# RWKV-7 scan with the tokens of two products stacked on 128 rows, the backward direction's stack in reverse order

## What is computed

```
def _wkv7_step(S, inp):
    r_t, w_t, k_t, v_t, aa_t, bb_t = inp
    sa = jnp.einsum('zbhij,zbhj->zbhi', S, aa_t)
    S = S * w_t[..., None, :] + sa[..., :, None] * bb_t[..., None, :] + v_t[..., :, None] * k_t[..., None, :]
    y = jnp.einsum('zbhij,zbhj->zbhi', S, r_t)
    return S, y
```

## Time and profile before

| | |
|---|---|
| median of 3 runs | 4864.06 us (4861.78 to 4869.06) |
| the profiled execution | 4869.98 us, its span 4867.9 us |
| busy shares over the span | PE 89%, PEld 74%, DVE 40%, ACT 27%, POOL 26% |
| matmul records in all | 50312 |
| the scan | first `lora` at 2491.8 us, last `y_products` at 3607.7 us |
| mean granted PE clock | 0.954 of 2.4 GHz |

### The profile page before, as it was taken

The page is one execution under the profiler, slowest core; times in us unless marked ns, Lnnn a source line. Parts: engine busy times, 40 slices in busy tenths (PEclk is TensorE's granted clock), DMA queues, the critical chain, the costliest instruction groups (busy, mean ns, idle before and its releaser), DMA issues. The chain is left out here.

```text
span 4867.9 us, 112762 instructions
## 1 busy us (share of the span) xinstructions
PE 4311.4 (89%) x50312; PEld 3614.9 (74%) x50312; DVE 1928.2 (40%) x3380; ACT 1292.7 (27%) x2542; POOL 1279.7 (26%) x794
## 2 busy tenths in 40 slices
PE   3899898999999996996958888888878999999997
PEld 2688856888888885885847777777755888888886
DVE  3011054154252443226146666666633244242441
ACT  1111065211011112236124444444422211011110
POOL 2111032311111115111125454555512311111110
PEclk8899999999999997998979999999989999999998
DMA  3211242311313112121232222221222311313214
GB/s 130 65 59 55 69 134 73 119 39 53 107 40 105 56 58 80 69 78 43 85 89 67 67 68 72 63 74 56 63 100 87 126 35 50 111 40 100 65 50 161
DMA packets 402639, 372.41 MB, mean 77 GB/s; under 512 B 63057, under 2 KB 370513, under 8 KB 399985
## 3 DMA queue, kind: packets, MB, share of 16 engines
q1 hardware_dynamic: 390320, 354.75, 23.6%
q10 hardware_dynamic: 11840, 10.49, 0.6%
HBM read 257.68 MB, written 107.48 MB: 75 GB/s over the span
## 5 line engine op out<-in xcount | busy, mean ns | idle before, releaser
L422 POOL TENSOR_TENSOR f_wlow<-f_raw,f_whigh 128x1024 fp32r<-128x1024 f32 (+1 forms) x152 | 360.1, 2369 | 1671.2 <-ACT f_whigh L493 1671.2
L478 PE MATMUL f_ps<-fx_hh,f_whigh 128*128 128x512 f32 (+1 forms) x2112 | 529.6, 359 | 0.0
L478 PE MATMUL f_ps<-fx_hl,f_whigh 128*128 128x512 f32 (+1 forms) x2112 | 528.5, 358 | 0.0
L478 PE MATMUL f_ps<-fx_hh,f_wlow 128*128 128x512 f32 (+1 forms) x2112 | 528.2, 358 | 0.0
L493 ACT ACTIVATE f_whigh<-f_raw 128x1024 fp32r<-128x1024 f32 (+1 forms) x152 | 156.6, 1030 | 922.7 <-PE f_ps L478 895.0
L478 PEld LDWEIGHTS f_ps<-fx_hl,f_whigh 128*128 128x128 f32 x2112 | 348.7, 189 | 65.8
L478 PEld LDWEIGHTS f_ps<-fx_hh,f_whigh 128*128 128x128 f32 x2112 | 348.5, 189 | 65.6
L478 PEld LDWEIGHTS f_ps<-fx_hh,f_wlow 128*128 128x128 f32 x2112 | 348.2, 188 | 65.7
L478 PE MATMUL f_ps<-mo_oh,f_whigh 128*128 128x512 f32 (+1 forms) x1440 | 360.8, 359 | 26.2 <-POOL f_wlow L422 26.2
L1605 PE MATMUL sc_inv_ps<-sc_tf,sc_bl 64*64 64x64 f32 x6400 | 283.0, 223 | 105.3 <-DVE sc_tf L1956 59.8
L478 PE MATMUL f_ps<-mo_ol,f_whigh 128*128 128x512 f32 (+1 forms) x1440 | 360.4, 359 | 0.0
(11 more groups left out here) (268 smaller groups left out, 8383.8 us busy)
## 6 DMA issues: line engine op xcount, KB each, us to landing
f_xo<-xres SPq DMA_DIRECT2D x64, 640.0 KB, 4.0
xres<-f_xo SPq DMA_DIRECT2D x56, 640.0 KB, 2.9
f_raw<-in_ffn_w_gate SPq DMA_DIRECT2D x44, 512.0 KB
f_raw<-in_ffn_w_up SPq DMA_DIRECT2D x44, 512.0 KB
sc_rk<-rkvl SPq DMA_DIRECT2D x80, 256.0 KB, 3.4
rkvl<-ri_ot SPq DMA_DIRECT2D x28, 640.0 KB, 2.9
f_raw<-in_ffn_w_down SPq DMA_DIRECT2D x32, 448.0 KB
qkv_raw<-in_na_w_qkv SPq DMA_DIRECT2D x24, 512.0 KB, 5.7
```

The source lines that it names most:

```text
L422: nc.gpsimd.tensor_tensor(wlow[:, m % 2, 0:kt], raw[:, 0:kt], whigh[:, m % 2, 0:kt].bitcast(F32), ALU.subtract).then_inc(cut_lo, 1)
L478: last = nc.tensor.matmul(ps[:, m % 2, n, 0:count], w[:, m % 2, k], x[:, k, t0:t0 + count], start=(k == 0 and w is whigh and x is xh), sto ...
```

## The change

All of it is in `rwkv_scan`. The rows that were multiplied in two products, one for each half, are stacked so that one product does both.

- `gram`: rows 0 and 1 of a block are the weights together (64 x 128), 8 products for each direction in place of 16. For the backward direction DVE and POOL write rows 0 and 1 in exchanged places, so that its stack is the other way round (`home(z)`, `away(z)`).
- `turn`: transposes by `nc.tensor.transpose`, of 64 x 128 at a time; the values are read with 64 columns of padding on one side (`vpad`), so that they land on rows `away(z)`. 16 calls for each direction in place of 24.
- `gx`, `sv`: 128-row stacks. `gx` holds the queries (or the masked query rows of the Gram matrix) and the masked read rows; `sv` holds the state and the values, and u and the values. `x_product` is then 4 products with 128 rows in place of 8 with 64, `s_product` 2 + 4 in place of 12, `y_products` 32 for each group in place of 48.
- The copies that fill the stacks are new work, most of it on ACT: `bm_copy` (two operations of 64 x 256 for each direction, unmasked; it stood on DVE), `query_copy` (four), `read_copy` (two), `turn_copy` with three operations of 512 columns in place of one of 512 and one of 256, `u_copy` with two in place of one.
- DVE: `gram_out` has two operations in place of three and waits for `a_bm`; `state_out` is two operations in place of one, the small product `pc` four in place of one.
- `y` comes out on its own rows, its store is two DMAs of a group in place of three, `yt` has two buffers in place of three.

The core of the diff:

```
-                    for s in range(U):
-                        u = unit(z, s)
-                        for a in range(2):
-                            for rows in halves:
-                                last = nc.tensor.matmul(gram_ps[rows, a, s * 128:(s + 1) * 128], rec[rows, r, z, u, a],
-                                                        rec[rows, r, z, u, 2:4].rearrange("p a n -> p (a n)"), start=True, stop=True)
+                    for u in range(U):
+                        for h, rows in enumerate(halves):
+                            last = nc.tensor.matmul(gram_ps[:, slot(h, z), u * 128:(u + 1) * 128], rec[rows, r, z, u, 0:2].rearrange("p a n -> p (a n)"),
+                                                    rec[rows, r, z, u, 2:4].rearrange("p a n -> p (a n)"), start=True, stop=True)
...
+                        for h, rows in enumerate(halves):
+                            nc.tensor.transpose(turn_ps[z][:, slot(h, z), u * C:(u + 1) * C], rec[rows, r, z, u, 0:2].rearrange("p a n -> p (a n)"),
+                                          ident[rows, rows])
+                        for h, rows in enumerate(halves):
+                            at = (z * W + u * C) if z == 0 else (C + W + u * C)
+                            last = nc.tensor.transpose(turn_ps[z][:, slot(h, z), W + u * C:W + (u + 1) * C], vpad[rows, r, at:at + 2 * C], ident[rows, rows])
...
+                        for h in range(2):
+                            last = nc.tensor.matmul(x_ps[side(h, z), z], gx[:, G % 4, z, slot(h, z), u, 0], sv[:, G % 2, 0, z, u, slot(h, z)],
+                                                    start=True, stop=True)
...
                     for z in range(Z):
+                        nc.tensor.matmul(s_ps[home(z), z], ident[home(z), home(z)], sv[home(z), G % 2, 0, z, unit(z, s)].rearrange("p q n -> p (q n)"),
+                                         start=True, stop=False)
+                    for q in range(2):
+                        for z in range(Z):
+                            u = unit(z, s)
+                            last = nc.tensor.matmul(s_ps[home(z), z, q * C:(q + 1) * C], t0[:, G % 2, z, q, u], sv[:, G % 2, 1, z, u, q],
+                                                    start=False, stop=q == 1)
...
+                        for h, rows in enumerate(halves):
                             for z in range(Z):
+                                r = rec[home(z), G % 4, z, u, 3] if h == z else rl[home(z), u]
+                                nc.tensor.matmul(y_ps[rows, z, to], sv[home(z), G % 2, 0, z, u, slot(h, z)], r, start=True, stop=False)
+                        for z in range(Z):
+                            for h, rows in enumerate(halves):
+                                q = slot(h, z)
+                                last = nc.tensor.matmul(y_ps[rows, z, to], sv[:, G % 2, 1, z, u, q], gx[:, G % 4, z, q, u, 1], start=False, stop=True)
...
+                    nc.scalar.activation(t0[:, G % 2, z].rearrange("p q u n -> p q (u n)"), turn_ps[z][:, :, 0:W], ACT.Copy)
+                    v = turn_ps[z][away(z), :, W:2 * W].rearrange("p q (u n) -> p q u n", n=C)
+                    nc.scalar.activation(sv[away(z), G % 2, 0, z].rearrange("p u q n -> p q u n"), v, ACT.Copy)
+                    nc.scalar.activation(sv[away(z), G % 2, 1, z].rearrange("p u q n -> p q u n"), v, ACT.Copy).then_inc(a_turn[z], 1)
...
+                        if s < 2 and group(I + 2):
+                            bm_copy(I + 2, s)
+                        if s == 0 and group(I + 1):
+                            query_copy(I + 1)
                         if s == 1 and group(I - 1):
                             y_copy(I - 1)
                         if s == 2 and group(I + 1):
                             turn_copy(I + 1, 0)
+                        if s == 3 and group(I):
+                            read_copy(I)
                         p_copy(I + 1, 3 * s + 2)
```

More of the change, by code:

```diff
@@ L1440, in rwkv_scan @@
         t_ps = [b[:, 256:512] for b in inv_ps]
-        x_ps, u_ps, s_ps = (chain_ps[:, :, i * C:(i + 1) * C] for i in range(3))
+        x_ps, u_ps, s_ps = chain_ps[:, :, 0:C], chain_ps[:, :, C:2 * C], chain_ps[:, :, 2 * C:4 * C]
         y_ps = low_ps[:, :, 0:W]
@@ L1466, in group, with slot, home, away @@
             return 0 <= G < NG
+        def slot(h, z):
+            return h if z == 0 else 1 - h
         def side(h, z):
-            return halves[h] if z == 0 else halves[1 - h]
+            return halves[slot(h, z)]
+        def home(z):
+            return halves[z]
+        def away(z):
+            return halves[1 - z]
         def uc(a):
@@ L1511, in store_y @@
                     sp.wait_ge(a_y, G + 1)
[L1512 to L1516, removed]
+                    for z in range(Z):
+                        c = col_of(z, j)
+                        sp.dma_start(ysc[:, p, z, c:c + W], yt[:, G % 2, z]).then_inc(y_stored[G % 2], 16)
                 for I in range(-4, NG):
@@ L1530, in _ @@
                 store_y(NG - 1)
-                for s in range(3):
-                    sp.wait_ge(y_stored[s], 48 * len(range(s, NG, 3)))
+                for s in range(2):
+                    sp.wait_ge(y_stored[s], 32 * len(range(s, NG, 2)))
                 for s in range(2):
@@ L1649, in x_product @@
                             pe.wait_ge(d_gram[z], G + 1)
+                        pe.wait_ge(a_al, G + 1)
                     for z in range(Z):
-                        for h, rows in enumerate(halves):
-                            nc.tensor.matmul(x_ps[side(h, z), z], ga[rows, G % 3, z, s], vt[rows, G % 2, z, s], start=True, stop=False)
-                    for z in range(Z):
-                        for h, rows in enumerate(halves):
-                            last = nc.tensor.matmul(x_ps[side(h, z), z], rec[rows, G % 4, z, unit(z, s), 2], st[rows, (4 * G + s) % (2 * U), z],
-                                                    start=False, stop=True)
+                        u = unit(z, s)
+                        for h in range(2):
+                            last = nc.tensor.matmul(x_ps[side(h, z), z], gx[:, G % 4, z, slot(h, z), u, 0], sv[:, G % 2, 0, z, u, slot(h, z)],
+                                                    start=True, stop=True)
                     last.then_inc(pe_x, 1)
@@ L1684, in y_products @@
                     pe.wait_ge(a_u, 4 * G + 4)
+                    pe.wait_ge(a_rl, G + 1)
                     if group(G + 4):
@@ L1881, in queries @@
                     nc.vector.tensor_tensor(rec[:, r, :, :, 2], uc(kk[:, G % 2]), ex0_of, ALU.mult)
-                    kept = strided(keep[:], j * U, [[NC + (NS - 1 - 2 * j) * U, Z], [1, U]])
-                    nc.vector.tensor_tensor(pc[:, r], ex_end, kept, ALU.mult).then_inc(d_rec, 1)
+                    for z in range(Z):
+                        c = (j if z == 0 else NS - 1 - j) * U
+                        for h, rows in enumerate(halves):
+                            ends = exb[rows, z, :, C if z == 0 else 0]
+                            last = nc.vector.tensor_tensor(pc[home(z), r, z, :, slot(h, z)], ends, keep[rows, z, c:c + U], ALU.mult)
+                    last.then_inc(d_rec, 1)
                 def bonus_out(G):
```

135 lines of the change are left out of this document (68 added, 67 removed).

## The result

The change made the kernel slower: 4932.49 us (4912.02 to 4936.35, 4 runs) against 4862.92 us (4856.61 to 4869.06) for the kernel before on the same chip, a ratio of 1.0132, 95% interval 1.0105 to 1.016. The profiled execution took 4936.17 us, its span 4934.2 us. The forecast was 4782 us; the time lies outside the range too.

The account below looks back on a forecast made before the run. The scan was taken as bound by instruction supply in dense stretches and latency elsewhere. A group: 26.7 - 3.0 (fetching) + 1.0 (walk) = 24.7 us; 41 x 2.0 = 82 us less, 4782 us; range from under 4745 to 4880 us.

Parts of the forecast that it names:

- Instructions: PE's instruction supply: 572 matmul records a group for 780, 4.5 packets, so 3.0 of 3.2 us of fetching come back.
- the walk without fetching: Step-by-step timeline of one group without instruction stalls: 23.5 us before the change, +1.0 us from the change.
- Rival 1: PE's instruction fetch: stalls shrink by less than half, 4905 us at worst; chance 0.08.
- PE's own work and the shapes: PE's matmuls in a group: 3.6 us saved against 4.8 us for 28 new changes of shape.
- rival 2: PE's 28 new shape changes cost more: gain gone from 0.28 us each, 4913 us at 0.35; chance 0.12.
- 64 rows or 128 I cost alike: ACT's copies: one of 256 columns holds ACT 0.28 us, one of 512 columns 0.48 us, whatever the rows.
- rival 3: ACT's queue decides: operations cost full length in steps 0 and 2, +1.4 us, 26.1 us a group, 4839 us; chance 0.2.
- the +1.2 us of DVE: DVE's work in a group: larger state_out operations and three tiny pc ones add 1.2 us on 18.
- Step 0: 0.0: Group's step 0: gram's -0.8 us offset by shape changes and DVE's wait for bm_copy, sum 0.0 us.
- There is no slack left on ACT: Step 0: with query_copy ahead, p_copy 2 ends at 6.9 us after x, just as late as the add (7.0).
- the walk's +1.0: Steps 0 to 3 of a group, without fetching: +1.0 us in sum, bounds +0.1 and +2.4.
- rival 5: PE's clock falls to 1.2 GHz for a tenth of the scan: +70 us, 4852 us; chance 0.05.

Follow-up runs that it names:

- experiments 3: The changed kernel with DVE's four small pc products moved behind bonus_out: 4956.94 us, ratio 1.0198 to the kernel before.
- experiment 4: The changed kernel with the four pc products moved to step 0 of the next iteration, with their own semaphore: 5009.06 us, ratio 1.0291 to the kernel before.
- experiment 1: The changed kernel with ACT's query copies moved from step 0 to step 1, ahead of y_copy: 4877.38 us, ratio 1.0032 to the kernel before.
- experiments 8 and 9: Changed kernel, query copies in step 1, y sorted by shape, unread products before lora and inverse: 4831.4 us; then pc behind inverse_init, none before lora: 4809.06 us.

## Why the prediction was wrong

The forecast had -2.0 us a group and the kernel took +1.7. Of the 3.7 us between them 1.8 are new waits and spans (+2.8 for +1.0), 2.4 are low clock and spread, which the sum had at nothing, and fetching gave back 0.4 more than forecast (the terms are rounded).

- **Instructions: right.** 3.0 us were to come back, 3.4 us did (spread included), and the walk without fetching began from 23.5 us where the medians give 23.4. Rival 1 fell.
- **PE's own work and the shapes: right, but for turn.** gram 0.89 us from first to last start for 0.85 predicted; s 0.55 for 0.55 to 0.6; y 2.48 for 2.6; a change of shape 0.153 us for 0.15 to 0.2, so rival 2 fell. The turns' 16 transposes take 0.49 us, not 0.9: they follow each other in 0.03 us, not at the pace of loads of 128 columns. Two turns gained 1.5 us where I had 1.0. None of this reached the end: the inverse behind the first turn now waits 1.1 us, and the first of step 3 waits 0.8 us longer.
- **The step that failed first: "64 rows or 128 I cost alike", 0.28 us for each ACT operation.** That price was the distance of two operations on all 128 rows, overlap included. On changing halves bm and query cost 0.39 and 0.43 us, together 2.51 us where the walk had 6 x 0.28 = 1.68. `turn_copy` takes 1.70 us where the walk had 3 x 0.48 = 1.44, and ACT's copy behind it, which the first inverse of step 3 waits for, has 0.02 us of idle time in front of it where it had 1.24 (medians):

```profile
3057.23 0.59 ACT L1790 ACTIVATE sc_t<-sc_low_ps 128x512 f32<-128x512 f32 x1
3057.83 0.59 ACT L1792 ACTIVATE sc_sv<-sc_low_ps 64x512 f32<-64x512 f32 x1
3058.33 0.58 ACT L1793 ACTIVATE sc_sv<-sc_low_ps 64x512 f32<-64x512 f32 x1
3058.93 0.28 ACT L1784 ACTIVATE sc_pt_last<-sc_inv_ps 128x128 f32<-128x128 f32 x1
```

DVE's operations on halves don't overlap either: two of `state_out` 0.55 us, four of pc 0.66. This is rival 3's mechanism, to which I had given 0.2 and 1.4 us (its 26.1 us a group is even what the medians give, though a part of that is the next point's); in steps 0 to 3 the waits before one inverse each grew by 0.2, 0.95, 1.1 and 0.8 us.

- **A wait that the walk didn't have: lora for `d_bonus`,** 1.0 us a group. I had counted the +1.2 us of DVE and said that what counts is where they stand in the queues, and then did not follow pc's place: ahead of `bonus_out`, whose bank lora writes. "Step 0: 0.0" fell by this 1.0 us alone; the medians give +0.7 with gram's gain in it. pc's place is 0.6 us of it (experiments 3 and 4). The trace shows a larger delay in the same queue. From `bonus_rows` (`sc_tb`) to `bonus_out` DVE takes 4.88 us in place of 3.13 (starts, medians of 40), with no idle time, and 0.96 of the 1.75 us is `bonus_rows` itself, 1.71 us in place of 0.75. Before the change it started 0.67 us after POOL's last operation had ended; now it starts just behind that operation's start and ends 0.55 us after its end. Before, then after:

```profile
3030.85 1.18 POOL L2014 TENSOR_TENSOR sc_rec<-sc_rk,sc_exb 128x512 f32<-128x512 f32 x1
3032.18 0.75 DVE L1868 SCALAR_TENSOR_TENSOR sc_tb<-sc_kd,sc_prm,sc_rk 128x512 f32<-128x512 f32 x1
```

```profile
3059.01 1.19 POOL L2055 TENSOR_TENSOR sc_rec<-sc_rk,sc_exb 128x512 f32<-128x512 f32 x1
3059.10 1.65 DVE L1906 SCALAR_TENSOR_TENSOR sc_tb<-sc_kd,sc_prm,sc_rk 128x512 f32<-128x512 f32 x1
```

Its inputs are in SBUF, as pc's in experiment 4, so this looks like that collision, brought in by the change; the walk had POOL at no cost. No kernel here moves `bonus_rows`, so its price on PE's path is not shown.

- **"There is no slack left on ACT"** was written in the walk, and it was the warning: query copies and the add were to end together, so an error on ACT stood on PE's path up to where DVE's chain came last, 0.4 us earlier in step 1 (experiment 1). With the terms above the walk's +1.0 became the +2.8 of the medians.
- **The clock: rival 5, given 0.05.** It said a tenth of the scan at 1.2 GHz and +70 us. From the first lora to the last y, low clock was 334 of 1184 us in the changed kernel, over a quarter, where it had been 54 of 1116; low clock and spread cost 2.4 us a group. I had rated it from a kernel whose longest wait for an engine was 1.0 us; the change took lora's gap from 0.15 to 1.2 us and the next long one, seven microseconds later, from 1.3 to 2.2 us, and the clock fell behind the second. I had treated the clock as independent of rival 3, though a walk that misses waits misses the clock with them.

The terms in sum: -3.4 + 2.8 + 2.4 gives +1.7 us a group before rounding, in place of -2.0.

Not settled: how the 2.8 us split between the lost overlap, `bonus_rows` beside POOL and the new order. No kernel here has bm and query on 128 rows, which the layout doesn't allow, so that overlap's share is shown as a cost on ACT and only argued as a cost on the path; experiment 1 shows that the query copies, overlap and all, are 0.4 us of it in step 1.

## What to carry to other kernels

Take the price of an operation from a neighbour with the same rows: one that overlaps its predecessor was cheaper by 0.1 us here than one on another half, and where a walk ends with two chains level, that 0.1 us can be on the path. A change that trades PE's work for waits can pay twice, as here, where PE's clock fell behind its idle time; fewer matmuls were a gain only once the waits were shorter or filled (experiments 8 and 9), and unread products in the gaps tell at once (here 71 us) whether clock is what is lost. An operation whose time shifts, be it small or not moved itself, must be looked at against what every other engine does at that moment: the same four products stood in waits of 1.0, 1.2, 2.1 or 0 us, by place.

## What was not expected of the hardware

- Stalls of PE at borders of 256 instructions and almost only there, 3.5 us apart at the densest: 104 of 106.
- ACT: 0.215 us between starts on the same rows, 0.304 us on changed rows, for the same 64 x 128 copy; from 128 rows to rows 0 to 63 the overlap stays.
- DVE against POOL: a 64 x 4 product with both inputs in SBUF lasted 1.9 us beside POOL's 2.9 us operation, 0.16 us otherwise; and `bonus_rows` 1.71 us beside POOL's 1.2 us operation, 0.75 us before the change.
- A met wait ahead of a matmul costs PE 0.1 us in a dense stretch.
- PE at 1.2 GHz in the middle of a busy phase, after gaps of 1.2 and 2.2 us with work between; six more products a group, in the gaps, kept 2.4 GHz in the middle of the scan and saved 71 us.
